# A fused decoder-layer step on one core: MLP down-projections as seven block products over a summed residual basis

## What is computed

```python
hm = _rmsnorm(x, g_mlp)
x = x + jnp.square(jax.nn.relu(hm @ w_up)) @ w_down      # w_up (1024, 4096), w_down (4096, 1024)
y = _rmsnorm(x, g_final)
```

## Time and profile before

| | |
|---|---|
| median of 3 runs | 2250.39 us (2249.12 to 2258.05) |
| the profiled execution, its own time | 2245.91 us |
| its span in the profile | 2244.1 us |
| mean granted TensorE clock | 0.996 of full speed |
| TensorE matmul busy | 2182.6 us, 97% |
| VectorE busy | 1065.8 us, 47% |
| ScalarE busy | 533.4 us, 24% |
| GpSimd busy | 440.1 us, 20% |
| DMA | 217.61 MB, mean 97 GB/s |

### The profile page before, as it was taken

How to read it: one execution, slowest core, us unless ns; L and a number is a source line. 1 busy time by engine, 2 the same in 40 slices (tenths; PEclk the granted TensorE clock), 3 DMA queues, 4 the chain that set the end, 5 groups by cost and what they waited for, 6 DMA issues and landing times. The chain is left out here.

```text
span 2244.1 us, 49247 instructions
## 1 busy us (share of the span) xinstructions
PE 2182.6 (97%) x21418; PEld 2061.6 (92%) x21418; DVE 1065.8 (47%) x1526; ACT 533.4 (24%) x1014; POOL 440.1 (20%) x368
## 2 busy tenths in 40 slices
PE   8999999999999999999999999998999999999997
PEld 6899888888888899989999987998999999999997
DVE  5333643636445355263544155466445445354455
ACT  4111433324333221153011023231102011011023
POOL 0233301112021022122333200321111111111110
PEclk9999999999999999999999999999999999999999
DMA  8446513424053074336113125111212122122122
GB/s 306 144 129 137 142 39 82 89 54 149 7 114 70 27 244 162 105 135 254 47 40 119 47 96 187 38 57 62 70 53 76 57 67 72 52 76 64 55 76 80
DMA packets 86663, 217.61 MB, mean 97 GB/s; under 512 B 10720, under 2 KB 26464, under 8 KB 83680
## 3 DMA queue, kind: packets, MB, share of 16 engines
q1 hardware_dynamic: 62944, 156.22, 21.0%
q0 software_dynamic: 12800, 33.56, 6.9%
q10 hardware_dynamic: 10752, 25.35, 3.2%
HBM read 187.04 MB, written 61.60 MB: 111 GB/s over the span
## 5 line engine op out<-in xcount | busy, mean ns | idle before, releaser
L517 PE MATMUL ps<-A_s,w_split 128*128 128x364 f32 (+1 forms) x3888 | 693.5, 334 | 1.9 <-ACT zstg L2250 1.9
L517 PEld LDWEIGHTS ps<-A_s,w_split 128*128 128x128 f32 x3888 | 643.5, 188 | 28.1 <-issue 12.5
L517 PE MATMUL ps<-hid,msp 128*128 128x364 f32 (+3 forms) x2304 | 388.3, 330 | 5.4 <-issue 5.4
L517 PEld LDWEIGHTS ps<-hid,msp 128*128 128x128 f32 x2304 | 385.1, 189 | 7.3 <-issue 6.0
L449 POOL CAST w_split<-w_raw 128x1024 fp32r<-128x1024 f32 x78 | 85.5, 1096 | 1117.0 <-PE ps L517 858.0
L517 PE MATMUL ps<-B_s,w_split 128*128 128x364 f32 (+1 forms) x1728 | 288.1, 328 | 0.4 <-POOL w_split L451 0.4
L517 PEld LDWEIGHTS ps<-B_s,w_split 128*128 128x128 f32 x1728 | 286.7, 188 | 0.7 <-issue 0.7
L1434 DVE TENSOR_TENSOR F<-ps,F 128x1092 f32<-128x1092 f32 (+3 forms) x84 | 104.3, 1241 | 352.3 <-PE ps L517 352.3
L509 POOL CAST msp<-mraw 128x512 fp32r<-128x512 f32 x176 | 115.1, 655 | 616.6 <-PE ps L517 604.0
L451 POOL TENSOR_TENSOR w_split<-w_raw,w_split 128x1024 fp32r<-128x1024 f32 x78 | 206.9, 2652 | 6.3
L517 PE MATMUL ps<-xb,msp 128*128 128x272 f32 x1536 | 200.2, 288 | 1.5 <-DVE F L1434 1.5
(11 more groups left out here) (249 smaller groups left out, 2408.4 us busy)
## 6 DMA issues: line engine op xcount, KB each, us to landing
w_raw<-w SPq DMA_DIRECT2D x80, 512.0 KB, 3.7
mraw<-w SPq DMA_DIRECT2D x112, 256.0 KB, 2.6
sums_up<-w POOLq DMA_DIRECT2D x24, 1024.0 KB, 9.4
mraw<-sums_up SPq DMA_DIRECT2D x64, 256.0 KB, 2.6
z<-zstg SPq DMA_DIRECT2D x83, 182.0 KB, 2.1
F<-z SPq DMA_DIRECT2D x16, 546.0 KB, 7.1
sums_up<-sums_up POOLq DMA_DIRECT2D x8, 1024.0 KB, 5.9
w_raw<-w SPq DMA_DIRECT2D x7, 1024.0 KB, 10.3
```

The lines of the kernel that those rows point to most:

```text
L517: return pe.matmul(out, lhsT, rhs, start=start, stop=stop, skip_group_check=skip)
```

## The change

Six of the eight stretches, all but the first (`o`, `d` = 0, 0) and the last (3, 1), get their down-projection as seven block products too (`mlp_fast`).

- The 512 hidden features, the 1024 output features and the 1088 tokens are each cut into two halves. A stretch's down-projection is 14 units (`FAST`: seven products, each for two pairs of output tiles) of 24 matmuls with 272 columns. Output tile pairs `t` 0 to 3 have PSUM banks 2t and 2t+1, and products 1, 2, 7, 3 (and 5, 4, and 6) go on adding in the same banks. After each unit VectorE reads two 544-column blocks out of PSUM and adds them to or takes them from one block of `F` (`read`).
- So that each product goes into one block only, two of the four blocks of `F` are kept as sums with a third one (`residual_in`, four instructions of 2176 columns in all): made between the quads of stretch (0, 1), undone between the quads of stretch (3, 1).
- The operands of the products are sums of hidden blocks. VectorE makes them (`tf`, `H12`, `H21`, 128 by 1088 each) and their lo parts (`lower`, `turned_lo`), ScalarE the hi parts (`turned_hi`). Some of the squares and lo parts of before go away: in such a stretch the first quad has no `hidden_lo`, the second has two.
- Sums of down weights are made in DRAM (`sums_down`) by 32 more steps of GpSimd's DMAs, behind splits 32 to 34 and 41 to 69. In two of the four groups each adding step is two DMAs. The loop of splits is written out.
- Units: a stretch has 28 (22 before), the loop's pair 56. Plain down weights come in runs of 256 values (1 KB) from two slots of `w`, where they came in runs of 512 values (2 KB).
- `acc_c` moves from PSUM banks 3 and 4 to 2 and 3.
- In the first stretch the order of VectorE's work at the end of the opening changes, and TensorE starts the first two output tiles when two `hid` lo blocks are there, hidden tile by hidden tile (0, 2, 1, 3), instead of at seven.

```diff
-        PAIR_UNITS = 44
+        PAIR_UNITS = 56
+        tf = at("tf", [P, 2, HT], oE + 4 * TB + 4 * ((NPAR + 7) // 8 * 8) + 512)[:, :, :]
+        FAST = [(p, u) for p in (1, 2, 7, 3, 5, 4, 6) for u in range(2)]
+        def mlp_fast(o, d):
+            return (o, d) not in ((0, 0), (3, 1))
-        acc_a, acc_b, acc_c = ps[:, 0:2, 0:HC], ps[:, 6:8, 0:HC], ps[:, 3:5, 0:HC]
+        acc_a, acc_b, acc_c, acc_m = ps[:, 0:2, 0:HC], ps[:, 6:8, 0:HC], ps[:, 2:4, 0:HC], ps[:, 3:5, 0:HC]
...
GpSimd
-            for n in range(XT + SIDE):
+            for n in range(XT + SIDE + S_CQ - S_MIX):
                 split(n, n % 2)
                 if n < 32:
-                    sum_step(n)
-            with pool.Fori(0, (S_MLP - S_MIX) // 2) as i:
-                for b in range(2):
-                    split(i * 2 + (S_MIX - S_PW + b), b)
+                    sum_step(n, 0, sum_block, up_block)
+                elif n < 35:
+                    sum_step(n - 32, 8, down_sum, down_block)
+                elif n >= 41:
+                    sum_step(n - 41 + 3, 8, down_sum, down_block)
...
TensorE
+            def down_first():
+                r = [mlp_ring(0, down_unit(0, 0, t)) for t in range(2)]
                 for t in range(2):
-                    if first and d == 0:
-                        pe.wait_ge(m_lo, BEFORE + 7)
-                        pe.wait_ge(m_b, BEFORE + 5 + t)
+                    pe.wait_ge(m_ready, mlp_units(0, 0, down_unit(0, 0, t) + 1))
+                    pe.wait_ge(m_lo, mlp_lows(0, 0, 0, 2))
+                    pe.wait_ge(m_b, BEFORE + 5 + t)
+                    down_part(r[t], t, (0,))
+                for k, n in ((2, 4), (1, 6), (3, 8)):
+                    pe.wait_ge(m_lo, mlp_lows(0, 0, 0, n))
+                    for t in range(2):
+                        last = down_part(r[t], t, (k,))
...
+            NEED = {1: 1, 2: 3, 7: 4, 3: 6, 5: 5, 4: 7, 6: 8}
+            def down_fast(i, o, d):
+                n = 4 * o + 2 * d + 2
+                for s, (p, u) in enumerate(FAST):
+                    l = down_unit(o, d, s)
+                    v, h = OPERAND[p]
+                    if u == 0:
+                        pe.wait_ge(m_lo, mlp_lows(i, o, d, NEED[p]))
+                    pe.wait_ge(m_ready, mlp_units(i, o, l + 1))
+                    for j in range(2):
+                        t = 2 * u + j
+                        if s >= 2:
+                            pe.wait_ge(m_f, mlp_reads(i, o, d, 4 * (s // 2 - 1) + t + 1))
...
+                        for k in range(2):
+                            for m, (wp, xp) in enumerate(((0, 0), (0, 1), (1, 0))):
+                                for c in range(2):
+                                    x0 = HT * h + HC * c
+                                    last = mm(ps[:, 2 * t + c, 0:HC], msp[:, mlp_ring(o, l), wp, 2 * j + k, :], hid[v][:, k, xp, x0:x0 + HC],
+                                              start=(p in (1, 7, 5, 6) and k == m == 0), stop=(k == 1 and m == 2), skip=p in (2, 3, 4))
+                    last.then_inc(m_used, 1)
...
VectorE, second quad of such a stretch ("odd")
+                if odd:
+                    squares_of(i, z0)
+                    own.add(tt(tf, H11, H12, ALU.subtract))
...
+                if odd:
+                    own.wait()
+                    lower(0, 0)
...
+                if odd:
+                    squares_of(i, z0 + 3)
+                    tt(H12, H12, H22, ALU.subtract).then_inc(t_sum, 1)
                 c.c21()
...
VectorE, the down-projection
+            def down_fast(i, o, d):
+                for s, (p, u) in enumerate(FAST):
+                    l = down_unit(o, d, s)
+                    v.wait_ge(m_used, mlp_units(i, o, l + 1))
+                    for t in (2 * u, 2 * u + 1):
+                        read(p, t)
+                    unit_lo(i, o, l + 4)
+                    if s == 0:
+                        turned_lo(H12, 0, 1, mlp_turns(i, o, d, 4, BEFORE_R + 5))
+                    if s == 2:
+                        turned_lo(tf, 0, 0, mlp_turns(i, o, d, 4, BEFORE_R + 6))
+                        v.wait_ge(m_lo, mlp_lows(i, o, d, 5))
+                        own.add(tt(tf, H22, tf, ALU.add))
+                    if s == 3:
+                        own.wait()
+                        lower(1, 1)
+                        own.add(tt(H21_hi, f32(hid[1][:, :, 0, 0:HT]), tf, ALU.subtract))
+                    if s == 4:
+                        own.wait()
+                        tt(H21, H21_hi, f32(hid[1][:, :, 1, 0:HT]), ALU.add).then_inc(t_sum, 1)
+                    if s == 6:
+                        turned_lo(H21, 1, 0, mlp_turns(i, o, d, 4, BEFORE_R + 7))
+                    if s == 10:
+                        turned_lo(tf, 0, 0, mlp_turns(i, o, d, 4, BEFORE_R + 8))
+            F12, F21, F22 = F[:, 0:8:2, HT:T], F[:, 1:8:2, 0:HT], F[:, 1:8:2, HT:T]
+            def residual_in(n, op1, op2):
+                v.wait_ge(m_f, n)
+                own.add(tt(F12, F12, F22, op1))
+                own.add(tt(F21, F21, F22, op2))
+                own.wait()
```

More of the change, by code:

```diff
@@ L463, in _, with put, plus, landed @@
             S1, S2, S3, S4 = range(4)
[L465 to L471 removed]
+            def put(g, dst, src):
+                pool.dma_start(dst, src).then_inc(d_sum[g], 16)
+            def plus(g, dst, src):
+                parts = [(dst[:, d], src[:, d]) for d in range(2)] if len(dst.shape) == 4 else [(dst, src)]
+                for x, y in parts:
+                    pool.dma_start(x, y, accum_op=ALU.add).then_inc(d_sum[g], 16)
+            def landed(g, before, puts, pluses):
+                pool.wait_ge(d_sum[g], 16 * (before + puts + pluses * (2 if before and g in (1, 2) else 1)))
+            def sum_step(n, before, to, block):
                 if n < 8:
[L474 removed]
+                    put(n // 2, to(n // 2, (S1, S3)[n % 2]), block(n // 2, *(A21, A11)[n % 2]))
                 elif n < 16:
@@ L500, in pair @@
+            for n in range(S_CQ - S_PW, S_MLP - S_PW):
+                split(n, n % 2)
+                sum_step(n - 41 + 3, 8, down_sum, down_block)
             def pair(i, o, first, last):
-                for l in range(PAIR_UNITS):
-                    pool.wait_ge(d_m[l % 4], i * 176 + (D_M + 176 * o + 16 * (l // 4) + 16))
-                    if first and l < 4:
+                for l in range(pair_units(o)):
+                    n, r = UNITS_BEFORE[o] + l, mlp_ring(o, l)
+                    pool.wait_ge(d_m[r], i * (4 * PAIR_UNITS) + (D_M + 16 * (n // 4) + 16))
+                    if n < 4:
@@ L1360, in down_part @@
                         for c in range(3):
-                            last = mm(down_bank(t, c), msp[:, l % 4, wp, k, :], hid[k // 2][:, k % 2, xp, real(c)],
-                                      start=(k == m == 0), stop=(k == 3 and m == 2), skip=True)
-                return last
-            def down(i, o, first, d, tiles):
-                z0, f0 = 16 * o + 8 * d, 16 * o + 8 * d
+                            last = mm(G[t % 2][:, c, 0:real(c).stop - real(c).start], msp[:, r, wp, k, :],
+                                      hid[k // 2][:, k % 2, xp, real(c)], start=(k == m == 0), stop=(k == 3 and m == 2), skip=True)
@@ L1394, in pair_of_groups @@
                         opening()
-                    else:
-                        quad(i, o, 2 * d)
-                        quad(i, o, 2 * d + 1)
-                    down(i, o, first, d, 6 if last and d == 1 else 8)
+                        down_first()
+                        down_rest(0, 0, 8)
+                        continue
+                    quad(i, o, 2 * d)
+                    quad(i, o, 2 * d + 1)
+                    if mlp_fast(o, d):
+                        down_fast(i, o, d)
+                    else:
+                        down_last()
+                        down_rest(3, 1, 6)
             pair_loop(pe, pair_of_groups)
@@ L2192, in down @@
+            def down(o, d, tiles):
                 for t in range(tiles):
-                    l = down_unit(d, t)
-                    v.wait_ge(m_used, i * PAIR_UNITS + (BEFORE + PAIR_UNITS * o + l + 1))
+                    l = down_unit(o, d, t)
+                    v.wait_ge(m_used, mlp_units(0, o, l + 1))
                     tt(tri(F[:, t, 0:T + 4]), G[t % 2], tri(F[:, t, 0:T + 4]), ALU.add).then_inc(m_f, 1)
-                    if not (last and d == 1 and t >= 4):
-                        unit_lo(i, o, l + 4)
@@ L2205, in pair_of_groups @@
                         opening()
-                    else:
-                        quad(i, o, 2 * d)
-                        quad(i, o, 2 * d + 1)
-                    down(i, o, d, 6 if last and d == 1 else 8, last)
-            QUAD_STEPS = 1
+                        down(0, 0, 8)
+                        continue
+                    quad(i, o, 2 * d)
+                    if first:
+                        residual_in(mlp_reads(0, 0, 1, 0), ALU.add, ALU.subtract)
```

(10 more changed lines are left out.)

293 lines of the change are left out of this document (186 added, 107 removed).

## The result

The changed kernel takes 2267.38 us (median of 4 runs, 2260.69 to 2268.91) against 2250.55 us beside it (4 runs, 2249.12 to 2258.05). The ratio is 1.0066, with a 95% interval of 1.0048 to 1.0084: it is slower by 0.66%. The forecast was 2228 us, faster, within 2211 to 2244; the measured time lies above that range and on the other side of the kernel before. The profiled execution took 2260.69 us, the fastest of the four, with a span of 2258.8 us.

A forecast was written before the change was run, and what follows sets the result against it. TensorE, busy 97%, was taken as the bound. Down-projections 16.8 plus opening 5.2 gave 22 us off the 2244.1 span, 2222; adding the offset of runs over span, 2228 us. Range of 8 in 10: 2211 to 2244.

The forecast's parts named there:

- what I cost at nothing: List of side costs taken as zero: residual passes, further unit loads, GpSimd's further DMA steps, bank wait, longer loop body.
- GpSimd's 32 further DMA steps behind splits: Ahead of the MLP: GpSimd's 6.4 us standstill covers the added DMAs; estimate 0, upper end 3 us in all.
- VectorE in the new down-projection: Six fast down-projections: 5.73 us less TensorE work a stretch, minus 2.9 us of new waits on VectorE; 17 us gained.
- collisions with casts: GpSimd casts meeting VectorE work with both inputs in SBUF: 0.41 us charged each, ends 0 and 0.62.
- crowded place: Early units of each fast down-projection, where VectorE's wide instructions fall; three cast collisions charged, waits of 1.1 and 1.3 us.
- rival 3: Units 0 to 7 of six down-projections: port makes VectorE the bound, waits 8.9 us a stretch; 2264 us, slower; 9%.
- The opening: End of the opening: first down-projection starts about 1540.1 instead of 1542.59, standstill 3.8 us; 5.2 us gained.
- the clock: TensorE's clock after the opening's 3.8 us standstill: taken to stay up, gain 5.2 us; if it falls, 2.5.
- The passes over the residual: Two VectorE passes between quads, 2 x 2 x 2.35 us, taken as covered; uncovered 0 to 5 us.
- six further loads a stretch: Unit loads on SP's queue, landing in 2.6 us, possibly double with 1 KB runs; costed at nothing.
- the bounds it names: Forecast's own range, stated as 2217 to 2239 us: collisions -7 and +6, clock +3.

The follow-up runs named there:

- 3: Changed kernel with the same forty summing DMAs issued singly: none behind splits 32 to 40, nine behind split 69; 2234.99 us, ratio 0.9936.
- 9: Changed kernel with summing DMAs one by one, VectorE's wide instructions one to a unit, and the opening's unit low parts sooner; 2219.33 us, ratio 0.9856.
- 6: Kernel before plus the forty unread summing DMAs, same places and bytes, in runs of 512 values instead of 256; 2261.96 us, ratio 1.0052.
- 5: Changed kernel with summing DMAs single and spread, but the first three copies kept behind splits 32 to 34; 2243.27 us, ratio 0.9973.
- 7: Changed kernel with summing DMAs single and spread, and VectorE's wide instructions in fast down-projections one to a unit; 2229.49 us, ratio 0.9908.
- 8: Changed kernel with summing DMAs single and spread, and the opening's low parts of units 14 and 15 made sooner; 2233.33 us, ratio 0.9918.
- 2: Changed kernel without its down-weight summing DMAs, fast loads reading the up-weight sums (wrong weights, equal size); 2230.67 us, ratio 0.9919.
- 4: Kernel before with only the opening's new VectorE order and earlier start of the first two output tiles; 2247.99 us, ratio 0.999.
- 10: Changed kernel with wide instructions spread and opening low parts sooner, without down-weight sums (wrong weights, equal size); 2219.88 us, ratio 0.9861.

## Why the prediction was wrong

**The step that failed** is the third under what I cost at nothing: "GpSimd's 32 further DMA steps behind splits", with "Twice as many descriptors, or two DMAs, have those 6 us as cover. Estimate 0; upper end 3 us in all." It measured 33.6 us (9.2 and 24.4) by the profile, and 33 by the ratios with and without the sums. What failed in it:

- The 6.4 us in which GpSimd stood still behind a summing DMA were cover for its next cast, but not for a second DMA. The same cast without a DMA ahead of it, in the kernel before, waits 8.41 us for TensorE, which is the 6.47 and the DMA's own 1.28 and 0.69 us together:

```profile
1064.17 1.04 POOL L449 CAST w_split<-w_raw 128x1024 fp32r<-128x1024 f32 x1 [8.41 <-PE ps L517]
```

- What I left out is that the next DMA can't leave before the last one has landed, 8 us or more after its issue. Two in a slot of 11.95 us need some 16.5, 4.5 too many, in each of the slots where a step is two DMAs; and four such slots stand in a row (splits 48 to 51). The page of the kernel before had a number for it that I did not use: `sums_up<-w`, 9.4 us from issue to landing, and twice that is more than a slot. The experiments agree: with one DMA in a slot the cost of the pairs went (3 and 9), and with fewer pieces in each it fell from 20.2 to 3.7 us (6).
- A part of the 33.6 us is not of this kind. At split 48, 4.6 us come from a load that is late beside the sums' transfers, and 4.2 to 8.0 with single DMAs (3, 5, 7 and 8). It is not there without sums (2, 4 and 10).
- The row of the DMA is 1.26 us long and says nothing of this. The Trainium skill (Perfetto Trace Analysis, DMA Instruction — SWDGE (GPSIMD)) states it: the end that the profiler shows for such a DMA is the end of making its descriptors, not of moving the data. The trace agrees, 1.26 us against 8.0 to landing.
- By the fit in the Trainium skill (DMA: Bandwidth & Descriptors, Anatomy of one DMA — SWDGE (gpsimd) path), 2.0 us and the bytes at 436 GB/s, 512 KB would take an estimated 3.2 us. The measured 8.0 decides: the fit does not hold for this accumulation between blocks of HBM.
- Of the three copies I had said nothing but that they are steps. They are not in the way of GpSimd's next DMA, but they came beside late loads and delayed those (8.3 us by the medians, experiment 5). The same loads are late by 0 to 6 us in profiles without copies, so the 9.2 us of the one profile are not theirs alone.

**VectorE in the new down-projection: right, and for its reasons.** 2.93 us of waits in a stretch where 2.9 were forecast, by place 0.94 (1.1), 1.26 (1.3), 0.58 (0.4 and 0.1) and 0.14. The collisions with casts are there, three in the crowded place of the stretch shown, as I had charged them. VectorE and GpSimd, after; the low part is usually 0.68 us, the cast 0.62:

```profile
1672.96 1.70 DVE L1531 TENSOR_TENSOR hid<-hidf,hid 128x1088 fp32r<-128x1088 f32 x1
...
1675.84 1.08 DVE L1531 TENSOR_TENSOR msp<-mraw,msp 128x512 fp32r<-128x512 f32 x1
...
1680.02 1.58 DVE L1531 TENSOR_TENSOR tf<-hidf,tf 128x1088 f32<-128x1088 f32 x1
```

```profile
1678.84 1.63 POOL L558 CAST msp<-mraw 128x512 fp32r<-128x512 f32 x1 [2.45 <-PE ps L566]
```

They cost VectorE 0.42, 0.40 and 0.30 us (against 1.28 and 0.68): what was left of a cast, never its whole 0.62, at which rival 3 stood. The fourth row is the other side, a cast that came behind a wide instruction and took 1.0 us longer. So the lock that the Trainium skill describes (SBUF — State Buffer, section SBUF: two separate sides) agrees with these four rows. What it does not give is how often the two meet: three times in the crowded place, because the instructions between read PSUM, and beside such a read the cast kept its 0.61 us (at 1681.83 in the same view). The forecast had that from the earlier trace rows. The size holds too: the six down-projections gained 15.8 us, 16.8 were forecast.

**The opening: the length right, the clock open.** A standstill of 3.45 us was measured where 3.8 was forecast. I took it as harmless; in some executions it is and in others it isn't (0.50 of the clock in experiment 4), so 5.2 us was the good case (5.0 in the profile of the change), and the usual one lies between it and 2.5 (3.4 to 3.7 in four profiles, 2.3 in experiment 4). What would have been safer is the shorter standstill of experiment 8.

**The other items at nothing.** The passes over the residual and the six further loads a stretch cost nothing that shows: no wait on a DMA in a stretch, and a load from `w`, some of them now in runs of 1 KB, lands in 2.7 us instead of 2.6. The loads from `sums_down`, in runs of 2 KB, take 3.0.

**The rivals.** Rival 3 named the sign, but not the mechanism: VectorE's port did not make it slower. The loss lay in a place for which the forecast had no rival at all. Its last line, "Wrong would be: waits at each unit (rival 3 or late loads), waits on GpSimd or on a DMA, a later start of the MLP", named what was seen, and no chance stood behind it. With the sums spread, the change as made gives 2235, within the range. One sum of the forecast doesn't come out, without bearing on this: the bounds it names (-7; +6 and +3) give 2221 to 2237, not 2217 to 2239, and no working stands behind the +6.

## What to carry to other kernels

Before adding DMAs to a queue, ask how long one of them holds the queue, and read this from the distance between two of them or from issue to landing, never from the length of their rows; a standstill behind a DMA can be cover for the engine's next instruction and yet none for a second DMA, while the first has not landed. Put such DMAs one to a gap that is longer than this, and the rest where nobody waits for that engine. Where instructions of an engine are late in one crowded place and idle beyond it, move the wide ones apart: here that gave 5.5 us for no work less.

## What was not expected of the hardware

- A DMA with accumulation of 512 KB from HBM to HBM in 528 packets kept GpSimd from issuing the next until 0.26 to 0.35 us after it had landed (7.7 to 9.0 us from issue to issue, over nine DMAs in a row), and casts behind the second one waited with it. A cast behind a single one did not. With pieces of twice the length (272 packets), two went out in 2.30 us, a third 6.4 us after the first, and the fourth stood for 16.23 us.
- A standstill of TensorE of 3.45 us left the granted clock at 1.00 in one execution and led to windows of 0.50 to 0.66 in five others, with the same instructions around it. After 5.37 us it fell, after 1.5 us it did not the earlier trace rows.
- Waiting costs TensorE twice: from 1040 to 1135 us there were 17.3 us of waits, and 24.4 us were lost; two of the three windows shown had a granted clock of 0.78 and 0.86.
- Three copies from HBM to HBM, issued from GpSimd between 699 and 800 us, cost 8.3 us by the medians (experiments 5 and 3): between 807 and 895 us loads of split weights on another queue came late.
- Eight loads of `F` and the summing DMAs at once: from 1038 to 1050 us 363 GB/s were moved, and two summing DMAs took 18.7 and 14.4 us to land where 8.0 is usual.
